# A hybrid decoder step on one core: turned copies first in the cross loop, sample values a step pair later, earlier splits of loads and norms

## The reference

```python
h = rmsnorm(x, g_mix) @ w_in                    # q | k | v | conv value | conv gate
att = dilated_attention(q, k, v, table)         # 12 heads of 64; samples also read 2048 cached keys/values
x = x + concat(att, conv_module(...)) @ w_out
mk, mv = rmsnorm(mem, g_mem) @ w_xk, ... @ w_xv # 256 memory tokens
q = rmsnorm(x, g_x) @ w_xq                      # 4 heads of 256
x = x + softmax(q @ mk.T / 16) @ mv @ w_xo      # samples use a cached mk, mv
x = x + (silu(h @ w_gate) * (h @ w_up)) @ w_down    # h = rmsnorm(x, g_ffn), inner width 2816
y = rmsnorm(x, g_final)
```

## Time and profile before

| | before |
|---|---|
| median of 3 runs | 2029.76 us (2029.33 to 2029.76) |
| the profiled execution: its time, its span | 2030.58 us, 2028.8 us |
| TensorE busy, mean granted clock | 94%, 0.983 |
| VectorE, ScalarE, GpSimd busy | 52%, 22%, 25% |

### The profile page before, as it was taken

One profiled execution on the slowest core, in us unless ns is written; L12 is line 12 of the kernel. 1 busy time (PEld: TensorE's weight loads), 2 busy tenths in 40 slices (PEclk: granted clock), 3 DMA queues, 4 the chain that ended last, 5 costly groups with the idle time before them and its releaser, 6 DMA issues. The chain is left out here.

```text
span 2028.8 us, 33274 instructions
## 1 busy us (share of the span) xinstructions
PE 1906.5 (94%) x13253; PEld 1764.3 (87%) x13253; DVE 1049.0 (52%) x2108; ACT 440.4 (22%) x902; POOL 508.5 (25%) x377
## 2 busy tenths in 40 slices
PE   6999996999999899899989999999999999999987
PEld 6999995666666799899648989999999999999987
DVE  6698635676666453512543354544544544544455
ACT  5000022555455421200431131001001001000005
POOL 2333221010100134452002223233332233333220
PEclk9999998999999999999999989999999999999998
DMA  4499958698888612124530123432433342311102
GB/s 150 141 339 339 311 177 205 158 212 212 212 208 220 182 42 73 52 84 147 175 105 21 47 70 132 166 124 83 165 124 113 144 161 86 124 42 47 46 21 89
DMA packets 221891, 281.38 MB, mean 139 GB/s; under 512 B 9409, under 2 KB 208457, under 8 KB 220041
## 3 DMA queue, kind: packets, MB, share of 16 engines
q1 hardware_dynamic: 221789, 279.95, 45.5%
HBM read 266.48 MB, written 113.89 MB: 187 GB/s over the span
## 5 line engine op out<-in xcount | busy, mean ns | idle before, releaser
L908 POOL CAST w_hi<-w_raw 128x1024 fp32r<-128x1024 f32 x98 | 105.3, 1075 | 980.2 <-issue 332.8
L1526 PE MATMUL bank<-g_lo,w_hi 128*128 128x362 f32 (+1 forms) x1056 | 350.4, 332 | 0.0
L1526 PE MATMUL bank<-g_hi,w_lo 128*128 128x362 f32 (+1 forms) x1056 | 350.3, 332 | 0.0
L1526 PE MATMUL bank<-g_hi,w_hi 128*128 128x362 f32 (+1 forms) x1056 | 347.8, 329 | 2.2 <-DVE g_lo L2454 2.2
L910 POOL TENSOR_TENSOR w_lo<-w_raw,w_hi 128x1024 fp32r<-128x1024 f32 x98 | 265.3, 2707 | 7.8
L1526 PEld LDWEIGHTS bank<-g_hi,w_hi 128*128 128x128 f32 x1056 | 199.7, 189 | 2.6 <-DVE g_lo L2454 2.5
L1526 PEld LDWEIGHTS bank<-g_hi,w_lo 128*128 128x128 f32 x1056 | 201.0, 190 | 0.0
L2531 DVE TENSOR_TENSOR xT<-bank,xT 128x362 f32<-128x362 f32 (+1 forms) x264 | 139.8, 534 | 116.2 <-PE bank L1546 116.2
L1526 PEld LDWEIGHTS bank<-g_lo,w_hi 128*128 128x128 f32 x1056 | 199.5, 189 | 0.0
L1546 PE MATMUL bank<-act_hi,w_hi 128*128 128x364 f32 (+1 forms) x528 | 176.3, 334 | 16.3 <-DVE xT L2531 10.2
L1546 PE MATMUL bank<-act_lo,w_hi 128*128 128x364 f32 (+1 forms) x528 | 174.2, 330 | 0.0
(11 more groups left out here) (289 smaller groups left out, 3651.3 us busy)
## 6 DMA issues: line engine op xcount, KB each, us to landing
out_sk_dram<-in_cache_win_k_dram SPq DMA_DIRECT2D x24, 2040.0 KB
out_sv_dram<-in_cache_win_v_dram SPq DMA_DIRECT2D x24, 2040.0 KB
vn<-in_cache_win_v_dram SPq DMA_DIRECT2D x24, 576.0 KB, 7.4
kb<-in_cache_win_k_dram SPq DMA_DIRECT2D x48, 256.0 KB, 5.4
vn<-in_cache_win_v_dram SPq DMA_DIRECT2D x24, 512.0 KB, 8.9
w_raw<-in_w_in_dram SPq DMA_DIRECT2D x22, 512.0 KB, 10.2
w_raw<-in_w_ffn_gate_dram SPq DMA_DIRECT2D x22, 512.0 KB, 3.8
w_raw<-in_w_ffn_up_dram SPq DMA_DIRECT2D x22, 512.0 KB, 3.8
```

What stands on the lines that cost most here:

```text
L908: pool.tensor_copy(w_hi[slot][:, :], w_raw[slot][:, :]).then_inc(w_hi_done, 1)
L1526: last = pe.matmul(out, w, r, start=start, stop=stop)
```

## The change

- **Cross loop.** ScalarE copies the turned `xp` of step v - 2 before the exponential of step v, and does the two roundings of a finished half after the parts beside it. V and W start one step pair later (from v = 18), so the last pair stands behind the last scores; ScalarE's wait for the stored memory keys moves into step 2.
- **Last unit.** Its first four far value tiles (1024 KB) are loaded at unit 9 into `d_strip` (`vn_early`), the rest at its turn. The last prompt values come before the turn of the last sample probabilities. x tiles 0 and 1 go to `kt01`, after the last unit's values; the weight tiles of unit 10 are loaded in units 2 and 3; the memory tiles and their gain go to `mk_nat` and `factor_x`.
- **Norms.** The second memory tile is turned two thirds of a group later. ScalarE copies the memory products beside Q 0 before it rounds the third group. Before the feed-forward part the last square and its addition come before the third group's split.
- **First gated tiles.** The first gate and up tile are multiplied group by group, both for one group before the next.

The diff, cut to its core:

```diff
+        EARLY = 4
+        vn_early = d_strip[:, 0:2 * EARLY * 2 * P].rearrange("p (b t c) -> p b t c", b=2, t=EARLY)
...
         number("P", STEPS - 1, 5)
+        number("O", STEPS - 1, 1)
         number("PS", UNITS - 1, 3)
-        number("O", STEPS - 1, 1)
...
-            elif n < 16:
-                parts.append(("W" if odd else "V", n - 8, 0))
+            elif 9 <= n < 17:
+                parts.append(("W" if odd else "V", n - 9, 0))
...
             def load_values(u):
-                load_far(cv_rows, vn, u, 0, FAR, vn_in)
+                if u == UNITS - 1:
+                    load_far(cv_rows, vn[:, :, EARLY:FAR, :], u, EARLY, FAR, vn_in)
+                else:
+                    load_far(cv_rows, vn, u, 0, FAR, vn_in)
...
-                if u == UNITS - 2:
+                if u in (2, 3):
+                    load_m(u + 1)
+                elif u == UNITS - 3:
                     sp_.wait_ge(d_made, 4)
                     sp_.wait_ge(dn_made, 3)
-                    load_x_again(0)
-                    load_x_again(1)
-                    load_m(3)
-                    load_m(4)
-
-
+                    load_far(cv_rows, vn_early, UNITS - 1, 0, EARLY, vn_early_in)
+
+
+            sp_.wait_ge(st_ready, 3 * UNITS - 1)
+            load_x_again(0)
+            load_x_again(1)
             keys_turned(UNITS - 1, 1)
...
+            f = FILL["OS", UNITS - 1, 0]
+            sp_.wait_ge(t_full[f % 3], f // 3 + 1)
             for t in range(2):
                 sp_.dma_start(mn[t], A["mem_prompt"][t * P:(t + 1) * P, :]).then_inc(m_in, 16)
-            sp_.wait_ge(sr_done, 3 * UNITS)
...
+                last_unit = u == UNITS - 1
+                pe.wait_ge(vn_in, 16 * VALUE_DMAS * (u + 1) - (16 * 4 if last_unit else 0))
+                if last_unit:
+                    pe.wait_ge(vn_early_in, 16 * 6)
...
+            values(STEPS - 1)
             turn_sample_p(UNITS - 1)
-            values(STEPS - 1)
...
-            MEMORY_BESIDE = {(2, 0, 1): 0, (2, 1, 1): 1}
+            MEMORY_BESIDE = {(2, 0, 1): 0, (2, 2, 0): 1}
...
+            def first_gate_up(n):
+
+                for g in range(3):
+                    pe.wait_ge(fn_lo, KC * (g + 1))
+                    for k in range(2):
+                        slot, use = weight_turn(n + k)
+                        if g == 0:
+                            pe.wait_ge(w_ready[slot], use)
+                        if (g, k) == (2, 1):
+                            pe.wait_ge(f_factor, 3)
+                        for _, out, w, r, start, stop in ffn_prods[0][k][3 * KC * g:3 * KC * (g + 1)]:
+                            last = pe.matmul(out, w, r, start=start, stop=stop)
+                        last.then_inc(*((f_ready, 1) if g < 2 else (w_used[slot], 1)))
+                        if (g, k) == (1, 0):
                             norm_sums(tools_f, 1)
-                    last.then_inc(w_used[slot], 1)
+                        elif (g, k) == (1, 1):
+                            norm_factors(tools_f, 1, FACTOR_BANKS)
...
+                if g == 2:
+                    for m in turned_beside(("Q", 0)):
+                        read_memory(m)
...
             square(tools_x, 0, KC // 2 - 1, 1)
-            for kind, j in M_TILES[M_TILES.index(("O", KC - 1)):]:
+            root(tools_x, 0)
+            for kind, j in M_TILES[M_TILES.index(("Q", 0)):]:
...
             for v in range(XU + 4):
-                if v < XU:
-                    act.wait_ge(xmx_done, 2 * v + 2)
-                    if v >= 2:
-                        act.wait_ge(xt_turned, v - 1)
-                        act.wait_ge(xn_done, 2 * (v - 1))
-                    act.activation(xp[v % 2][:, :], bank[v % 2][:, 0:NM], ACT.Exp, bias=xmx[:, v % 2:v % 2 + 1],
-                                   accum_out=xrs[:, v % 2:v % 2 + 1]).then_inc(xe_done, 1)
...
+                if v < XU:
+                    act.wait_ge(xmx_done, 2 * v + 2)
+                    if v >= 2:
+                        act.wait_ge(xt_turned, v - 1)
+                        act.wait_ge(xn_done, 2 * (v - 1))
+                    act.activation(xp[v % 2][:, :], bank[v % 2][:, 0:NM], ACT.Exp, bias=xmx[:, v % 2:v % 2 + 1],
+                                   accum_out=xrs[:, v % 2:v % 2 + 1]).then_inc(xe_done, 1)
...
+                if v >= 4 and (v - 4) % 4 == 3:
+                    hf = (v - 4) // 4
+                    for c in range(2):
+                        act.wait_ge(xv_ready, 2 * hf + c + 1)
+                        act.activation(g_hi[:, 2 * (hf // 2) + c, 512 * (hf % 2):512 * (hf % 2) + 512],
+                                       bank[3 + c][:, :], ACT.Copy).then_inc(xv_hi, 1)
...
+                if g == 2:
+                    square(tools_f, 1, KC // 2 - 1, 1)
...
+                if g == 2:
+                    add_square(tools_f, 1, KC // 2 - 1, 1)
```

More of the change, by code:

```diff
@@ L192, in layer_step @@
         s_kv.close()
-        halves = [d_strip[:, i * D:(i + 1) * D] for i in range(2)]
+        kt_flat = kt01[:, :, :].rearrange("p g n -> p (g n)")
+        halves = [kt_flat[:, 0:D], kt_flat[:, D:2 * D]]
         for i in range(2):
@@ L238, in layer_step @@
         s3a.close()
+        mn = [mk_nat[:, t, :] for t in range(2)]
+        g_mem = factor_x[:, 0:D]
         s3c = ExitStack()
@@ L346, in layer_step @@
         vn_in = sem("vn_in")
+        vn_early_in = sem("vn_early_in")
         sc_ready = sem("sc_ready")
@@ L542, in beside_step @@
                 parts += [("K", n, 2 * odd), ("K", n, 2 * odd + 1)]
-            elif n < 16:
-                parts.append(("W" if odd else "V", n - 8, 0))
+            elif 9 <= n < 17:
+                parts.append(("W" if odd else "V", n - 9, 0))
             return parts
         XFILL = {}
-        for v in range(XU):
+        for v in range(XU + 2):
             for part in beside_step(v):
@@ L1194, in sample_values @@
                         c = member(u, g)[0]
-                        keys = vn[:, g % 2, t, member_columns(g)] if t < KT else vs_nat[:, c * P:(c + 1) * P]
+                        place = vn_early if last_unit and t < EARLY else vn
+                        keys = place[:, g % 2, t, member_columns(g)] if t < KT else vs_nat[:, c * P:(c + 1) * P]
                         last = pe.matmul(out[32 * g:32 * g + 32, 0:P], pT_s[:, t, 32 * g:32 * g + 32], keys,
@@ L1509, in gate_up @@
             def gate_up(n, i=None):
-                for k in range(4):
+                if i is None:
+                    first_gate_up(n)
+                for k in range(2 if i is None else 0, 4):
                     slot, use = weight_turn(n + k, i, 6)
@@ L1516, in gate_up @@
                     for g, out, w, r, start, stop in products:
-                        if start and i is None and k == 0:
-                            pe.wait_ge(fn_lo, KC * (g + 1))
-                        if start and i is None and k == 1 and g == 0:
-                            norm_factors(tools_f, 1, FACTOR_BANKS)
-                        if start and i is None and k == 1 and g == 2:
-                            pe.wait_ge(f_factor, 3)
                         ev = 3 * (first_ch + k // 2 - 1) + g + 1
@@ L1528, in gate_up @@
                             last.then_inc(f_ready, 1)
-                        if stop and i is None and k == 0 and g == 1:
+                    last.then_inc(w_used[slot], 1)
+            def first_gate_up(n):
[11 more added lines that the diff above has]
+                        if (g, k) == (1, 0):
                             norm_sums(tools_f, 1)
-                    last.then_inc(w_used[slot], 1)
+                        elif (g, k) == (1, 1):
+                            norm_factors(tools_f, 1, FACTOR_BANKS)
             def down(n, i=None):
@@ L1729, in _ @@
                     act.wait_ge(m_step, 2 * t)
-                act.activation(factor_x[:, 0:D], mn[t], ACT.Square, accum_out=m_ssq[:, t:t + 1]).then_inc(m_step, 1)
+                act.activation(tools_x["sq"][0][:, 0:D], mn[t], ACT.Square, accum_out=m_ssq[:, t:t + 1]).then_inc(m_step, 1)
                 act.wait_ge(m_step, 2 * t + 1)
@@ L1750, in root @@
                                    scale=1.0 / D).then_inc(n_rms, 1)
+            act.wait_ge(m_step, 4)
             def memory_hi(t):
@@ L1813, in _ @@
             act.wait_ge(w_used[slot], use)
[L1814 removed]
             for v in range(XU + 4):
[L1816 to L1822 removed]
+                if v == 2:
+                    act.wait_ge(mk_out, 16)
                 if 2 <= v < XU + 2:
@@ L1831, in _ @@
                        .then_inc(xt_done, 1)
-                if v >= 4 and (v - 4) % 4 == 3:
-                    hf = (v - 4) // 4
-                    for c in range(2):
-                        act.wait_ge(xv_ready, 2 * hf + c + 1)
-                        act.activation(g_hi[:, 2 * (hf // 2) + c, 512 * (hf % 2):512 * (hf % 2) + 512],
-                                       bank[3 + c][:, :], ACT.Copy).then_inc(xv_hi, 1)
+                if v < XU:
```

(9 more changed lines are left out.)

7 lines of the change are left out of this document (removed).

## The result

The changed kernel takes 2009.09 us (median of 4 runs, 2003.37 to 2015.77) where the kernel before takes 2029.76 (4 runs, 2029.33 to 2033.91): ratio 0.990, 95% interval 0.9877 to 0.9923. The forecast was 2004, range 1994 to 2013, and faster. The profiled execution took 2011.81, its span is 2010.0, 18.8 less than before; the sum said 25.5. Repeated later, the changed kernel gave 0.9893 (0.9868 to 0.9917).

What follows compares the result with a forecast made beforehand. TensorE, busy 94% of the span, was taken to bound the kernel, so only its idle or low-clock time could go. 33.7 us off and 8.2 on, net 25.5, gave 2004 us, range 1994 to 2013.

Steps and rivals of the forecast that it cites:

- the five places: Attention's end, memory turn, first query tile, first gated tiles, cross loop: nearly all TensorE idle time considered, 33.7 us off.
- What it adds, 1024 KB ahead of unit 10's keys: Attention, unit 10: early values queued ahead delay the keys by 4.5 us at 232 GB/s; fallen clock 2.0 more.
- The 512 KB at unit 3: Attention: weight loads moved to unit 3 delay unit 4's keys, adding 2.3 us.
- End of the attention: Last unit to third output group: earlier values let VectorE's rests end sooner, 4.8 us off (4.4 to 7.4).
- Memory turn: Second memory tile's turn: wait for m_lo falls from 3.88 to 1.2, clock stays up, 4.3 us off.
- First query tile: Wait of 5.96 goes, a new one of 2.9 comes before the norm's sums; with the clock 5.7 us off.
- the term for the clock: First query tile: the low clock from 828 to 834 goes, 2.6 of the 5.7 us.
- The second rival: Improved places: shorter waits still bring the clock down, 1.6 + 2.6 + 1.6 and half of 4.5 not won, 2012 us; chance 0.22.
- First gated tiles: Feed-forward start: two waits and the low clock go, a new wait of 0.3 comes, 9.1 us off.
- Cross loop: Waits for turned cache keys and xp_T shrink, sample values move to the loop's end, 9.8 us off.
- Nothing elsewhere: Outside the five places: the span does not change, 0 us.

Runs made afterwards that it cites:

- q_norm_first: Changed kernel with the last square, its addition and the first memory copy ahead of the third group's work at the first query tile: 2003.94 us, ratio 0.9855.
- early_u10: Changed kernel with the 1024 KB of early values issued at unit 10, behind its values, instead of unit 9: 2005.21 us, ratio 0.9862.
- keys_first: Changed kernel with the early values issued one load later, behind unit 10's third keys instead of ahead of them: 2006.14 us, ratio 0.987.
- order_only: Kernel before with only the last prompt values ahead of the turn of the last sample probabilities, no early loads: 2031.8 us, ratio 1.0016.

## Why the prediction was right, and where it was not

The direction, the five places, and the total within its range were right; the net of 25.5 was 18.8 in the profile and about 21 in the medians. In part that is luck: the attention up to unit 11 and the first query tile came out 12.2 us worse than forecast, and the end of the attention and the cross loop 4.7 better. By the steps of the prediction:

- **What it adds, 1024 KB ahead of unit 10's keys: mis-sized.** Forecast +4.5, measured +9.1 in the profiled execution and 5.8 and 6.1 in two others. The mechanism holds (the last tests: 512 KB cost 2.2, the same bytes one place later under 1). The step that failed is the rate: I divided by 232 GB/s, read from a stretch without the loads. The same stretch of the changed kernel, from the issue of the strips to the arrival of the keys:

```profile
611.30:642.30 31.00, 20.79 (x256) 16.02 (x244) 13.03 (x51) 12.86 (x28) 1.54 (x8) 0.89 1.06 204
```

  Before it was 22 us at 232 GB/s, 5.1 MB; here it is 31.0 us and 6.3 MB. At 204 the 5.1 MB alone need 3.0 us more, and the 1.2 MB more that went here need 6.0. In the two other executions the rate over this stretch was 216 and 226 GB/s, so that less of the price is the rate and most of it the bytes. With 512 KB it was 229. Why the rate differs between executions isn't shown.
- **The 512 KB at unit 3: right (+2.3, measured +2.9), but its clock was left out.** The wait grew to 4.14 (3.10 to 4.43 in the six other traces with this load there), and the clock fell behind it: 2.0 more. The forecast counted a fallen clock only at unit 10 (+2.0, measured 1.3). A wait of 0.94 at unit 8 (0.23 before) wasn't forecast either.
- **The Trainium skill** (DMA: Bandwidth & Descriptors, section Queues, rings and completion order) has a queue's descriptors taken in ring order. The runs agree: a wait of 1.01 with the keys ahead of the early values, 6 to 9 with them behind. SyncE's issue instructions for the early values themselves take 8.9 us there (5.74 + 3.19).
- **End of the attention: -4.8, measured -7.3**, the end of the range that supposed undisturbed rests. The third group's rests could start 4.3 earlier, as forecast (counted from the same scores: 24.2 us instead of 28.5). For their length I took the row of before, 6.65 for eight rests beside GpSimd's split; the split began only at 702.53, and the rests took 3.66. The clock of this place (0.52 and 0.59 before, 1.00 after) was not named: the working took 2.14 for 36 matmuls that ran at half clock before, and so had its first half in it. The second half, 1.5 over the sample values, went into a new wait of 1.50 for the first group's rests. The order alone gave nothing.
- **Memory turn: -4.3, measured -4.1.** 1.25 waited (1.2 forecast), clock up.
- **First query tile: -5.7, measured -0.8.** The new wait was as forecast (3.44, forecast 2.9), and named with its cause. What failed is the term for the clock: I took 2.6 as won though the wait that stays was nearly as long as the 3.88 behind which it fell in the earlier trace rows. It fell again, and lasted longer, until 844; why longer isn't shown. Five other traces with this order are up to 1.4 better here than the profiled one, which is still far from 5.7. The second rival describes this place; it was right here and, but for a few microseconds behind the first gated sums, wrong at the other three. q_norm_first shows it: without that wait 3.8 to 5.2 come back.
- **First gated tiles: -9.1, measured -8.1** here and -9.9 alone. The sums were ready, but the clock fell behind them in the changed kernel's profile: 0.83 over the ten microseconds from their start, which costs 1.7, about the difference between the two.
- **Cross loop: -9.8, measured -12.0.** The `ckt` waits went (2.6). The waits for `xp_T` left less behind than the 3.2 in the middle that I took from one row: VectorE's new waits are 0.77, three times 0.42, and 0.73 at the end. At the end of the loop the clock stayed at 1.00.
- **Nothing elsewhere**: within 0.2 between the places; the last 740 us were 1.1 shorter, and the first 327 0.7, about what these stretches vary by.

## What to carry to other kernels

A load moved earlier is paid by whatever stands behind it in its queue: look up which load that is, whether something else already stands ahead of it (here the bias strips, in every second unit), and put the moved load behind the urgent one, if only by one place. Price the bytes by the rate of a full stretch with such loads in it, with a margin, not by the best one nearby. When a wait is replaced by a shorter one, read for each what the clock did behind a wait of the length that is left: in these traces it was down behind 2.13, 2.36 and 3.44, and up behind 1.25 and 1.50 (exceptions stand in the last section). And move what the next matmuls need (here one square and one addition of 1.1 and 1.3 us) ahead of a whole group's splits.

## What the runs showed of the hardware that was not expected

- VectorE's rests with two SBUF operands take 583 ns beside an idle GpSimd and up to 2734 beside its splits, 2.15 us more, which is most of one split (2.41 to 2.57). The trace's row for those of the first query tile (minimum, median, maximum):

```profile
L2378 DVE SCALAR_TENSOR_TENSOR g_lo<-xT,gains,g_hi x24: 583/590/2734, 809.8 to 831.9; 128x362 fp32r<-128x362 f32 x16, 128x364 fp32r<-128x364 f32 x8
```

  Eight of them took 4.16, 9.99 and 6.22 us in the three groups. The Trainium skill (SBUF — State Buffer, section SBUF: two separate sides) says that the two lock each other out for whole instructions; the maximum agrees, more clearly than the 6.65 of the earlier trace rows did. Part of VectorE's lateness before the norm's sums is this; that wasn't tried apart.
- The same two early loads took SyncE 5.74 us to issue and ScalarE 1.1 (0.43 + 0.70) on its own queue, which held nothing else. With both queues in use the engines moved 239 to 279 GB/s from 615 to 635, against 196 to 243 in the changed kernel; one execution of each.
- Behind the 18 products with one column, which keep TensorE busy for 2.04 us, the clock can fall with no wait right before them. At the first gated sums it read 0.83 over the ten microseconds from their start in five of the nine traces with the new order, and 1.00 in four. early_u10 and keys_first have the same order there and differ in this. What decides it stays open.
- The length of a wait doesn't decide it alone either: behind the 2.83 at 695.11 of the kernel before the clock stayed at 1.00, and behind the 2.87 at 698.75 of order_only it read 0.66 over 699 to 704.
